# TensorE's steps put in order by the shape of their weights, and the prompt's logits of two pairs of heads issued one behind the other

## The reference

```python
for l in range(DEPTH):                                   # DEPTH = 2
    q, k, v, qi, ki, wi, ga, xb, gb, u, vc, gc = project(xp, pos_p, norm_pre[l], w_in[l])   # rmsnorm, then h @ w_in
    ya = prompt_sparse_attention(q, k, v, qi, ki, wi)    # indexer scores, top-128 keys, softmax, values; 8 heads x 64
    yb, pst = pool_mix(xb, zeros, pos_p, pool_w[l], pool_scale[l])      # windows 2, 4, 8, 16 of the last rows
    yc, _ = sgu_mix(u, vc, sgu_w[l], sgu_b[l], sgu_norm[l])             # masked 128 x 128 mix of the rows of a chunk
    xp = merge(xp, ya, yb, yc, ga, gb, gc, w_out[l], norm_post[l])      # gates, @ w_out, rmsnorm, residual
    # the same for the sample rows, with keys and values gathered from the paged cache, top-256
    ya = sample_sparse_attention(q, k, v, qi, ki, wi, cache_k, cache_v, cache_kidx, page_table, l)
```

## Time and profile before

| | |
|---|---|
| runs | 1000.43, 1005.8, 1006.95 us, median 1005.8 |
| profiled execution | 1003.58 us, of which the span of its instructions is 1001.9 us; mean granted TensorE clock 0.997 |
| PE | 958.4 us busy (96%), 5948 matmul records |
| DVE | 533.6 us busy (53%) |
| ACT, POOL | 308.9 us (31%), 272.6 us (27%) |
| DMA | 205.06 MB, 205 GB/s over the span |

### The profile page before, as it was taken

How to read it: one execution, slowest core, us unless ns; L and a number is a source line. 1 busy time by engine, 2 the same in 40 slices (tenths; PEclk the granted TensorE clock), 3 DMA queues, 4 the chain that set the end, 5 groups by cost and what they waited for, 6 DMA issues and landing times.

```text
span 1001.9 us, 18229 instructions
## 1 busy us (share of the span) xinstructions
PE 958.4 (96%) x5948; PEld 484.6 (48%) x5948; DVE 533.6 (53%) x1706; ACT 308.9 (31%) x690; POOL 272.6 (27%) x484
## 2 busy tenths in 40 slices
PE   5999999999999999999999999999999999999996
PEld 4634444444444555655564444444444455555543
DVE  4439997564883233323344599965568632432232
ACT  4121132422233344433222211234212424453312
POOL 8710223222222222304432022323232222241110
PEclk9999999999999999999999999999999999999999
DMA  9841867677757564847475147766667566665551
GB/s 316 163 162 38 291 231 251 205 248 231 261 177 273 194 213 147 309 138 235 153 234 153 55 155 269 239 226 212 245 236 254 187 225 246 197 224 196 168 179 52
DMA packets 91945, 205.06 MB, mean 205 GB/s; under 512 B 15047, under 2 KB 26550, under 8 KB 91858
## 3 DMA queue, kind: packets, MB, share of 16 engines
q0 software_dynamic: 38944, 123.98, 36.9%
q1 hardware_dynamic: 47778, 75.78, 22.5%
q10 hardware_dynamic: 5136, 4.20, 1.4%
HBM read 193.87 MB, written 10.14 MB: 204 GB/s over the span
## 4 chain that ended last, share of the span: by engine, by line
PE 82%; DMA 5%; ACT 5%; DVE 4%; issue 2%; ACTq 1%; SPq 1%; POOL 0%; POOLq 0%; DVEq 0%
PE bank L1442 37%; PE bank L1770 11%; PE bank L1494 5%; PE bank L1459 5%; PE bank L1426 5%; DMA pg<-in_cache_k_dram 4%; PE bank L1699 2%; PE bank L1663 2%; PE bank L1707 2%; PE bank L1592 2%; PE bank L1517 2%; PE bank L1543 1%; PE bank L1554 1%; DVE r L1354 1%; DMA wr<-in_w_in_dram 1%
## 5 line engine op out<-in xcount | busy, mean ns | idle before, releaser
L1442 PE MATMUL bank<-wr,ht 128*128 128x512 f32 (+1 forms) x1024 | 435.9, 579 | 5.6 <-DVE ht L1159 1.9
L1442 PEld LDWEIGHTS bank<-wr,ht 128*128 128x128 f32 x1024 | 189.5, 190 | 221.8 <-issue 203.3
L675 POOL DMA_DIRECT2D wr<-in_w_in_dram x50 | 37.3, 746 | 304.6 <-PE bank L1442 260.1
L692 POOL DMA_DIRECT2D pg<-in_cache_v_dram x128 | 69.8, 545 | 154.2 <-PE bank L1494 128.0
L692 POOL DMA_DIRECT2D pg<-in_cache_k_dram x128 | 69.6, 544 | 69.7 <-PE bank L1459 48.8
L1077 DVE TENSOR_SCALAR_CACHE_REDUCE r<-r,sel_i 128x1088 bf16<-128x1088 f32 x62 | 82.8, 1336 | 0.0
L1459 PE MATMUL bank<-pg,qbx 128*32 128x256 f32 x1024 | 63.8, 383 | 6.7 <-DMA pg<-in_cache_k_dram 3.3
L1426 PE MATMUL bank<-wr,ht 128*64 128x256 f32 (+1 forms) x576 | 66.5, 385 | 2.1 <-DVE ht L1159 1.5
L1172 DVE CUSTOM_DVE_ANT_0 r<-bank,r 128x256 f32<-128x256 f32 (+2 forms) x48 | 24.9, 555 | 80.3 <-PE bank L1699 79.9
L1494 PE MATMUL bank<-pg,rs 128*32 128x256 f32 x1024 | 62.1, 382 | 0.2 <-DMA pg<-in_cache_v_dram 0.2
L1770 PE MATMUL bank<-wr,qt 128*128 128x512 f32 x128 | 59.1, 604 | 0.6 <-ACT r L1008 0.6
(11 more groups left out here) (268 smaller groups left out, 1157.3 us busy)
## 6 DMA issues: line engine op xcount, KB each, us to landing
pg<-in_cache_k_dram SPq DMA_DIRECT2D x128, 256.0 KB, 5.3
pg<-in_cache_k_dram POOLq DMA_DIRECT2D x128, 256.0 KB, 5.9
pg<-in_cache_v_dram SPq DMA_DIRECT2D x128, 256.0 KB, 5.1
pg<-in_cache_v_dram POOLq DMA_DIRECT2D x128, 256.0 KB, 5.9
wr<-in_w_in_dram POOLq DMA_DIRECT2D x40, 512.0 KB, 4.2
wr<-in_w_in_dram POOLq DMA_DIRECT2D x6, 1024.0 KB, 6.2
wr<-in_w_in_dram POOLq DMA_DIRECT2D x2, 2048.0 KB, 15.7
wr<-in_w_out_dram POOLq DMA_DIRECT2D x8, 512.0 KB, 4.1
```

Source lines behind the costliest of these rows:

```text
L675: pool.dma_start(W[n % 2][:, k, d0:d0 + w], src[k.start * P:k.stop * P, c0:c0 + w].rearrange("(k p) n -> p k n", p=P))\
L692: pool.dma_start(PG[2 * gi + e], cache[l, bass.ds(nos[2 * gi + e], 1), :, :].rearrange("o p n -> p (o n)"))\
L1442: mm = pe.matmul(b[0:m, 0:w], HT[:, k, rt * P:rt * P + m], W[n % 2][:, k, 0:w], start=(k == 0), stop=(k == KC - 1))
```

## The change

Five parts per tile take the place of four: `FRONT` (128x128 steps), `ROWS_A` (64-row steps), `COLS` (32-column steps), `ROWS_B`, `BACK`. Steps move among them so that those of one weight shape follow each other, and products are recast so that fewer shapes occur:

- `sample_product`, `PV`, the pooling products, and the sample's `sg`, `py`, `sgus` use weights of 32 columns, twice as many instructions, four side by side instead of two (`sg`, `py` and `sgus` of the sample two instead of one).
- `mk` multiplies with 128-row weights (`REPX`, made by a new DVE step `rep` per pair), the last `turn` and the sample's part of `V` with 128 rows.
- `L` of two pairs of heads stand behind each other at every second tile; `P` moves to the front of its tile, both heads share a bank for i < 2, and for i >= 2 the second head's transposes are a step of their own (`P2`).
- `S` of the new keys (j = 2) and its `H` stand with j = 0; `kis` and `whx` move a tile later; `OUTS` and `RES` put the sample's two output tiles next to each other.
- `turn` steps move to the back of the tile before their `V` (`TURNS_AT`), the masks by `MASKS_AT`.

```diff
-OUTS = ((0, 0), (1, 0), (0, 1), (1, 1), (2, 0), (2, 1), (3, 0), (ST, 0), (3, 1), (ST, 1))
-RES = (0, 1, 2, 3, ST)
+OUTS = [((0, 0), (1, 0), (0, 1), (1, 1), (2, 0), (2, 1), (3, 0)) + ends
+        for ends in (((ST, 0), (ST, 1), (3, 1)), ((3, 1), (ST, 0), (ST, 1)))]
+RES = ((0, 1, 2, ST, 3), (0, 1, 2, 3, ST))
+AHEAD_OF_SAMPLE = (20, 29, 34, 39)
+TURNS_AT = ((20, 0, 0, (0,)), (20, 4, 0, (1,)), (21, 4, 0, (2,)), (22, 4, 0, (4, 3)),
...
-    slots = [([], [], [], []) for _ in tiles]
-    FRONT, PAGE_, MID, END = range(4)
+    slots = [([], [], [], [], []) for _ in tiles]
+    FRONT, ROWS_A, COLS, ROWS_B, BACK = range(5)
...
-    put(s0, END, *[("S", 0, p) for p in range(PAIRS)], ("H", 0), *[("S", 1, p) for p in range(PAIRS)])
+    put(s0, BACK, *[("S", j, p) for j in (0, 2) for p in range(PAIRS)], ("H", 0), ("H", 2), *[("S", 1, p) for p in range(PAIRS)])
...
-    put(s0 + 1, END, ("sgus",), ("H", 1), *[("S", 2, p) for p in range(PAIRS)], ("H", 2))
+    put(s0 + 1, COLS, ("H", 1))
...
+    put(s0 + 10, FRONT, ("rep", 0), ("rep", 1))
+    heads = [n for n in range(25, 42) if n != 29]
+    for m, ((i, c), n) in enumerate(zip(HPAIRS, heads)):
+        n = heads[m | 1]
+        put(n, ROWS_A if n + 1 in AHEAD_OF_SAMPLE else ROWS_B, ("L", i, c))
+        put((heads + [42, 43])[m + 2], FRONT, ("P", i, c))
...
-    for m, (i, c) in enumerate(HPAIRS):
-        n = 25 + m if m < 4 else 26 + m
-        put(n, END, ("L", i, c), ("E", i, c))
-        put(n + 1, MID, ("P", i, c))
-        put(n + 2, MID, ("PV", i, c))
+    for m, ((i, c), n) in enumerate(zip(HPAIRS, heads)):
+        put(heads[m | 1], BACK, ("E", i, c))
+        put((heads + [42, 43])[m + 2], COLS, ("PV", i, c))
...
             def sample_product(b, lhs, weights, w):
                 for k in range(KC):
                     for t in range(2):
-                        mm = pe.matmul(b[t * NS:(t + 1) * NS, 0:w // 2], lhs(k), weights[:, k, t * (w // 2):(t + 1) * (w // 2)],
-                                       start=(k == 0), stop=(k == KC - 1), skip_group_check=True)
+                        for r in range(0, NS, 32):
+                            r0 = t * NS + r
+                            mm = pe.matmul(b[r0:r0 + 32, 0:w // 2], lhs(k)[:, r:r + 32],
+                                           weights[:, k, t * (w // 2):(t + 1) * (w // 2)],
+                                           start=(k == 0), stop=(k == KC - 1), tile_position=(0, r0), skip_group_check=True)
...
                 for kb in range(i + 1):
                     for t in range(2):
-                        mm = pe.matmul(pvp_banks[i % 2][part, c * P:(c + 1) * P], V[:, kb, h * HD:(h + 1) * HD],
-                                       PTS[2 * (m % 2) + t][:, kb * P:(kb + 1) * P], start=(kb == 0), stop=(kb == i),
+                        for r in range(0, HD, 32):
+                            r0 = t * HD + r
+                            d0 = 2 * c * HD + r0
+                            mm = pe.matmul(pvp_banks[i % 2][r0:r0 + 32, c * P:(c + 1) * P], V[:, kb, d0:d0 + 32],
+                                           PTS[2 * (m % 2) + t][:, kb * P:(kb + 1) * P], start=(kb == 0), stop=(kb == i),
+                                           tile_position=(0, r0), skip_group_check=True)
...
-                    pe.matmul(b[:, 0:w], REP[rows_, t, :], MSK[rows_, c0:c0 + w], start=True, stop=True,
-                              tile_position=(32 * p, 0)).then_inc(dve_full, 1)
+                    pe.matmul(b[:, 0:w], REPX[p % 2][:, t, :], MSK[:, c0:c0 + w], start=True, stop=True).then_inc(dve_full, 1)
...
-                    for t in range(2):
-                        b = act_bank(*s, t)
+                    b = act_bank(*s, 0)
+                    for t in range(1 if i >= 2 else 2):
```

More of the change, by code:

```diff
@@ L269, in _layer @@
-    put(43, END, ("ldsmall",), ("xl", ST), ("xl", 2), ("xl", 3))
-    put(45, MID, ("gaS",))
+        put(33 + n, COLS if rt == ST else FRONT, ("sg", rt))
+        n = at["xg", rt]
+        put(n + 1, COLS, ("pl", rt))
+        put(n + 2, COLS if rt == ST else FRONT, ("py", rt))
+        if rt != ST:
+            put(n + 3, FRONT, ("yT", rt))
+    put(34, BACK, ("silu", "ga"))
+    for i, n in enumerate((34, 35, 38, 42)):
+        put(n, BACK, ("gs", i))
+    for i, n in enumerate((35, 37, 40, 44)):
+        put(n, FRONT, ("gT", i))
@@ L271, in _layer @@
+    put(38, BACK, ("xl", 0), ("xl", 1), ("gpost",))
+    put(43, BACK, ("ldsmall",), ("xl", ST), ("xl", 2), ("xl", 3))
+    put(45, ROWS_A, ("yT", ST), ("gaS",))
+    for n, part, p, js in TURNS_AT:
+        if (n, part) == (38, FRONT):
+            put(n, part, *[("turn", p, j) for j in js])
+    for (i, c), n in zip(HPAIRS, heads[2:] + [42, 43]):
+        if i >= 2:
+            put(n, FRONT, ("P2", i, c))
     if l + 1 < DEPTH:
         for n in range(4):
-            put(46 + n, END, KEY_STEPS[n][:1] + KEY_STEPS[n][2:], layer=l + 1)
+            put(46 + n, BACK, KEY_STEPS[n][:1] + KEY_STEPS[n][2:], layer=l + 1)
@@ L274, in _layer @@
         for s, n in zip(POOL_KEYS, (45, 45, 46, 46, 47, 48, 49)):
[L275 to L281 removed]
+            put(n, BACK, s[:1] + s[2:], layer=l + 1)
+    last = {rt: n_out + max(m for m, o in enumerate(OUTS[l]) if o[0] == rt) for rt in RTP}
@@ L282, in _layer @@
+    for rt in RES[l]:
+        put(last[rt], ROWS_B, ("res", rt))
+        if l + 1 < DEPTH and rt != 3:
+            put(last[rt] + 1, ROWS_B, ("norm", rt), layer=l + 1)
+            if rt != ST:
                 put(last[rt] + 2, FRONT, ("xT", rt), layer=l + 1)
@@ L319, in _act_uses, with _last_turned @@
     if kind == "P":
-        return [s + (t,) for t in range(2)]
+        return [s + (0,)]
+    if kind == "P2":
+        return [("P",) + s[1:] + (1,)]
     return []
+def _last_turned(l, i, c):
+    return ("P", l, i, c, 1 if i >= 2 else 0)
 def _dve_uses(s):
@@ L1577, in pooled @@
+                        for g, r in four:
+                            mm = product(g, r, ZA[:, rt, :], BAND[:, :, 16:P], 16, P - 16, start=True, stop=True)
+                    else:
+                        for g, r in four:
+                            product(g, r, ZA[:, rt, :], BAND, 0, P, start=True, stop=False)
+                        for g, r in four:
+                            mm = product(g, r, ZA[:, rt - 1, :], PREV, 0, 16, start=False, stop=True)
                 mm.then_inc(dve_full, 1)
```

257 lines of the change are left out of this document (136 added, 121 removed), and 3 rows, old and new, of the table TURNS_AT.

## The result

The changed kernel takes 1017.46 us in the median of four runs (1014.74 to 1019.76), the kernel before 1004.23; the ratio is 1.0127, with a 95% interval of 1.0106 to 1.0147. The forecast was 988.5, within 976 to 1001. The profiled execution took 1018.61 us, with a span of 1016.9, so the profiles stand 15.0 us apart.

The account below looks back on a forecast made before the run. PE, busy for 96% of the span, was taken as the bound. From the profiled 1003.58 us, -17.9 - 8.0 - 9.0 + 12.4 + 5.6 + 2.0 = -14.9 gave 988.7, stated as 988.5, range 976 to 1001.

Parts of the forecast that it names:

- A: PE's list over both layers: fewer changes of weight shape, 402 before and 210 after, -17.9 us.
- B: PE's list: fewer entries into a weight shape that show a weight load, -8.0 us.
- G: Products split into 32-column weights: twice the instructions, but four side by side take the time of two, 0 us.
- H: `mk` with 128-row weights and the `rep` steps on DVE: 4 per layer and small, 0 us.
- D: Two pairs' logits: the fourth product waits until DVE has emptied the first's bank, +12.4 us, bounds 0 and about 20.
- R1: Rival, chance .16: the fourth logits product's wait costs nothing, 976.1 us.
- C: PE's stalls at the layer boundary, indexer scores, `kis` and `P` go, -9.0 us.
- F: `P2` and the sample's z transposes: about six PE stalls for ACT's copies, +2.0 us.
- E: `K` and `V` page steps, tiles 33-34 and 38-39: intervals shrink but loads get no quicker, +5.6 us.
- R2: Rival, chance .18: page loads and DVE give the gain back, 998.3 us.
- R4: Rival, chance .04: at tiles 26 and 28 logits wait 7.5 us for DVE's top-k chunk, +30, 1018 us.
- The sign that I gave for being wrong: PE's idle time rises by more than A to C save, or a shape change costs under 0.09 when fewer remain.

## Why the prediction was wrong, by its steps

- **A and B, right.** -25.9 was forecast, -27.8 is the model's difference, and the price itself held in a run made for it (1.0181 against 1.018). The trace has the 210 changes that were counted ahead (weights of 120 rows taken as 128).
- **G and H, right.** The split costs nothing (ratio 1.0008), and no line of `mk` or `rep` is among the waits. Of the two figures of the Trainium skill that I weighed (TensorE: Matmul & The Clock Gate, section "Wait — 56ns, not 53.3ns?"), the 62 ns for a small matmul with hardware decode off is out: `PV` is busy for 38.8 ns a record. The floor of about 25 ns from start to start is not borne out either where four products stand side by side: the 32 records of L1613 at 418.93 us start within 0.67 us, 21 ns each in the mean, and the measurement decides.
- **D, right in kind, near in size.** 14.2 against 12.4. The 512-column case is exact (0.96 us, four times), and 128 columns came to 0.56 to 0.94 where 0.54 was taken. The second doubles of 256 and 384 columns were put too low, 1.19 and 1.09 where 0.73 and 0.85 were taken; at 256 the third product waits too, until DVE's gating (L1250) has emptied its bank. The rival R1 is out: the run with the pairs apart saved 13 to 14 us.
- **C failed, as a whole, and most of all: it is the step that had the wrong sign.** Of "stalls that go", -9.0, the three that stand by themselves (boundary, scores, `kis`) were put at -4.6 and came to +5.8; the fourth, -4.4 for `P`, did come, as `P` is no longer in the list of waits, but `P2`'s waits came in its place (F). I priced the wait that each move took away, and not what the moved step would then meet. "`kis` a tile later: 0.32 twice, -0.7" failed most: in a round of two banks, the third of three steps in a row waits for DVE's turn, which hung on ACT's gathers. The scores' reordering took away the 2.5 us of work that hid a weight load (+2.7). At the layer boundary the wait of 1.48 us for DVE became one of 1.99, by the times for ACT, which was issuing gathers for 4.18 us; no run tests this one.
- **F was mis-sized.** "About six of them, +2.0" by the earlier trace rows. The nearest row was ACT's plain copy with 0.34 us; behind an output tile ACT makes two passes, and behind an `xg` tile it loads a table for 1.28 us. There are six of them, as counted, but of 0.85 to 0.99 us each; with those of turns and tiles the group grew by 8.6 us where I had -4.4 + 2.0.
- **E, right in kind, little over half in size.** 10.0 (9.0 by the named waits) against 5.6. The K step at tile 34 waits in both halves (1.48 and 0.85 us), where I had counted on slack for half of it; and the loads for V at tile 39 were 2.03 and 0.57 us late.
- **The clock, not in the sum at all.** The prediction has no term for it. Four stretches followed new or longer waits, +3.9 us net by the table, +5.4 step by step. That the start-up's stretch comes with its wait is shown: it is there in every profile with a wait of 4.2 to 4.9 us ahead of `qis` (also in the kernel before with that one move) and in none without. For the shorter waits it is not.
- **The rivals.** None was what happened. R2 had the right place for a part of it (the loads), but the idle time for K and V, 11.1 us, stayed under the 12 of the forecast, and the mechanisms that cost more were others. R4's 1018 is near the measured time by chance: its chunk of the top-k never stood between, and no double waits 7.5 us. None of the four held the sum of small new waits that decided it: C was taken at full value, E at a little over half, F at about a third (2.0 for six waits that show 5.5 us), and the clock at nothing, so that all large errors went one way. The range ended at 1001 because E and F had no upper bound beyond the nearest row, and C none at all.
- **The sign that I gave for being wrong.** "PE's idle time rises by more than A to C save" (34.9 us) did not show, though the prediction was wrong: idle time rose by 25.5 us. Most of D's wait and all that the half clock costs count as busy time in the profile, so the sign was set on the wrong quantity.

What stays open: the part of the page loads in layer 0 at tile 38 to 39 (2.03 us, 0.77 in layer 1), what decides whether half clock follows a wait of 1 to 3 us, and how the loss divides among the smaller lines of the table, of which only the sum is tested.
